# Weight products of a hybrid recurrent decoder as three fp32r products with split tiles, and heads issued in pairs

## The chip, the cores and the metric

The kernel runs on one core of a Trainium2 chip. The metric is the device time of one execution in microseconds; the median of several executions counts.

## The reference, cut to what matters

A decoder of two layers works on 288 token columns: 256 of a prompt and 32 of 8 sample sequences of 4 tokens each, which come with stored states. The model width is 1024, all in fp32. Each layer does this (cut; `prm` holds the weights):

```
u   = rmsnorm(h, norm_mix)
z   = u @ w_in                      # columns of four mixers, and of their merge gates mg
oa  = GLA(z), ob = RetNet(z), oc = gated DeltaNet(z), od = Mamba-2 SSD(z)   # chunked recurrences
proj  = einsum('blnv,nvd->blnd', stack(oa, ob, oc, od), w_branch)
gates = sigmoid(mg.reshape(B_, L, 4, D_MODEL))
h  += sum(gates * proj, axis=2) @ w_out
u   = rmsnorm(h, norm_ffn)
h  += (silu(u @ wg) * (u @ wu)) @ wd          # layer 0: one dense block of 2816
h  += top-2-of-8 experts of the same shape    # layer 1
h  += sigmoid(rmsnorm(h, norm_ple) @ ple_w_gate) * (p[i] @ ple_w_proj)   # layer-input gate
```

Besides the output, the new states of the four mixers are returned for the prompt and for every sample sequence.

## The kernel before

Activations lie transposed: 128 rows of a model block on the partitions, the 288 tokens along the free axis, `KD` = 8 such blocks. Every weight comes in tiles of 128 x 1024 fp32 (512 KB), each of which feeds eight matmuls of 128 x 128 weights by 288 columns into one PSUM bank. `TABLE` lists the tiles in the order in which they are used: for a layer 46 tiles `z` (input columns of the mixers GLA, RET, GDN and SSD: 12, 12, 12 and 10), 32 `mg` (merge gates, 8 for each mixer), 16 `br` (branch projections, 4 for each) and 8 `out`; then in layer 0 22 pairs `gate` and `up` and 22 `down`; at the end of each layer 2 `pproj` and 8 `pgate`. The 528 tiles of the experts are streamed by code of their own, which already splits each tile into a high and a low fp32r part (ACT copies it to fp32r, DVE subtracts that from the tile) and multiplies with three products (L1199 to L1201, L1221 to L1223).

Nothing is scheduled by a compiler. Each engine has its own instruction list, and semaphores tie them together. SP starts the load of tile t into slot t % `RING` of a ring of 11 slots, as soon as PE has used tile t - 11 (`tile_done`). PE does a mixer's recurrence step by step; where a step has to wait for the other engines, it fills in weight tiles. The table `SLOTS` says how many tiles stand at each of these places, and `fill(L, n, s)` issues them on PE (`stream`, matmul at L696 for z, mg, pgate and out, at L703 for br) and, at the same place of their own lists, on ACT (`take`, which copies the bank out: L1291 to L1299) and on DVE (`branch_tile`, L1598 and L1601, which multiplies br banks by their gates). So all three engines are in order, and a wait at the head of one list holds all that stands behind it. Tile t uses bank t % 2 of PSUM, so PE may start tile t when tile t - 2 is taken.

While RET's tiles run, br tiles of the mixer before (GLA) are filled in, and so on: the first places of each mixer hold the four br tiles of the last one. GDN and SSD begin with a convolution on DVE (four operations L1786 to L1792 for one block of 128 channels) and ACT (L1397, a tanh for each block), 8 blocks in GDN and 6 in SSD; the transposes on PE (L783) can only begin behind it.

For one head, `outputs(hh)` in `core` issues three matmuls of the prompt and then, for each of the 8 sample sequences, one with the head's 64-row state as weights and 4 columns (L834). GLA, RET and GDN put the even head of two in rows 0 to 63 of the array and the odd head in rows 64 to 127; SSD's two heads of a pair share the rows and write other output columns. `states(L, n)` does, head by head, two prompt matmuls (L881, L882) and eight of 32 x 64 by 128 (L889) with masks that POOL has written (L2252), or in SSD one of 512 columns (L886). GDN's `ks` products (L1020) have 4 columns too.

## Time and profile before

| | |
|---|---|
| median of 3 runs | 2867.82 us (2862.18 to 2868.1) |
| profiled execution | 2866.38 us |
| its span | 2864.4 us |
| mean granted TensorE clock | 0.922 of 2.4 GHz |
| busy: PE, DVE, ACT, POOL | 2684.9, 1309.7, 826.8, 169.4 us |
| matmul records | 12532 |

The busy time of an engine is the union of its instructions' times. An fp32 matmul appears as two records in the trace, so a tile of eight matmuls has 16 records, while an fp32r matmul has one. The granted clock is 1 at 2.4 GHz and 0.5 at 1.2 GHz.

### The profile page before, as it was taken

To read this page: it belongs to the slowest core of one execution; us is meant where nothing else is said; L and a number is where in the kernel's file an instruction comes from. 1 tells how busy PE (TensorE), PEld (TensorE's weight loads), DVE (VectorE), ACT (ScalarE), POOL (GpSimd) and SP (SyncE) were. 2 spreads that over 40 slices of the span, in tenths; PEclk is the share of its full clock that TensorE was granted. 3 is DMA by queue.
4 is the path that set the end of the run, shared out by engine and by line. 5 is a ranking of instruction groups with operands and counts; after the bars stand their busy time and mean duration, and the time that the engine had idled before them with its cause. 6 is when DMAs were issued, how large, how long until landed. Compare 5 with 4: busy or idle time off the path is not lost.

```text
span 2864.4 us, 34373 instructions
## 1 busy us (share of the span) xinstructions
PE 2684.9 (94%) x12532; PEld 2133.0 (74%) x12532; DVE 1309.7 (46%) x1790; ACT 826.8 (29%) x1171; POOL 169.4 (6%) x245
## 2 busy tenths in 40 slices
PE   8999979899999999999979899989999999999997
PEld 6777757777677776777757777668788788787785
DVE  1231252153311022132253243348879778888883
ACT  1110111012000001110111011026667666666661
POOL 0200101011100000110001010100000000000000
PEclk8989989788999998998889878879999999999999
DMA  5213321021334342323231121139889888898872
GB/s 218 96 67 119 113 73 59 30 93 48 112 125 138 134 138 82 110 74 105 81 112 59 37 71 52 51 144 335 300 309 322 305 329 300 309 341 290 306 284 85
DMA packets 122256, 455.29 MB, mean 159 GB/s; under 512 B 14024, under 2 KB 14442, under 8 KB 119730
## 3 DMA queue, kind: packets, MB, share of 16 engines
q1 hardware_dynamic: 118818, 433.51, 42.7%
q0 software_dynamic: 3344, 20.41, 1.9%
q8 instruction: 72, 1.18, 0.2%
q14 instruction: 22, 0.18, 0.0%
HBM read 442.87 MB, written 11.00 MB: 158 GB/s over the span
## 4 chain that ended last, share of the span: by engine, by line
PE 82%; DVE 10%; issue 5%; ACT 2%; DVEq 0%; DMA 0%; ACTq 0%; POOL 0%; POOLq 0%
PE ps L696 27%; PE ps L1098 6%; DVE weights_low L2093 4%; PE ps L1199 4%; PE ps L703 3%; PE ps L1201 3%; PE ps L1200 3%; PE ps L1105 3%; PE ps L834 3%; PE ps L1221 3%; PE ps L1222 3%; PE ps L1223 3%; PE ps L1172 3%; PE ps L889 2%; PE ps L726 1%
## 5 line engine op out<-in xcount | busy, mean ns | idle before, releaser
L696 PE MATMUL ps<-u,ring 128*128 128x288 f32 x2752 | 756.6, 437 | 10.8 <-DVE u L1612 7.9
L696 PEld LDWEIGHTS ps<-u,ring 128*128 128x128 f32 x2752 | 558.7, 206 | 179.9 <-issue 17.9
L2093 DVE TENSOR_TENSOR weights_low<-ring,weights_high 128x1024 fp32r<-128x1024 f32 x528 | 609.9, 1217 | 44.7 <-ACT weights_high L1507 40.6
L1507 ACT ACTIVATE weights_high<-ring 128x1024 fp32r<-128x1024 f32 x528 | 514.0, 1052 | 98.4 <-PE ps L1201 49.4
L1199 PE MATMUL ps<-weights_high,rows_high 128*128 128x512 f32 (+1 forms) x768 | 294.5, 383 | 28.0 <-DVE weights_low L2093 27.6
L1201 PE MATMUL ps<-weights_high,rows_low 128*128 128x512 f32 (+1 forms) x768 | 285.6, 372 | 0.0
L1200 PE MATMUL ps<-weights_low,rows_high 128*128 128x512 f32 (+1 forms) x768 | 285.1, 371 | 0.0
L1199 PEld LDWEIGHTS ps<-weights_high,rows_high 128*128 128x128 f32 x768 | 144.1, 188 | 62.6 <-DVE weights_low L2093 44.0
L1098 PE MATMUL ps<-u,ring 128*128 128x288 f32 x704 | 172.6, 409 | 3.2 <-DVE u L1612 3.2
L1098 PEld LDWEIGHTS ps<-u,ring 128*128 128x128 f32 x704 | 134.7, 191 | 41.1 <-issue 3.6
L1201 PEld LDWEIGHTS ps<-weights_high,rows_low 128*128 128x128 f32 x768 | 144.1, 188 | 20.9
L1200 PEld LDWEIGHTS ps<-weights_low,rows_high 128*128 128x128 f32 x768 | 144.4, 188 | 18.8
L703 PE MATMUL ps<-arena,ring 128*128 128x288 f32 x512 | 138.5, 431 | 9.3 <-DVE arena L1598 9.3
L1221 PE MATMUL ps<-weights_high,hidden_high 128*128 128x512 f32 x352 | 138.5, 394 | 0.0
L1222 PE MATMUL ps<-weights_low,hidden_high 128*128 128x512 f32 x352 | 137.0, 389 | 0.0
L1223 PE MATMUL ps<-weights_high,hidden_low 128*128 128x512 f32 x352 | 137.0, 389 | 0.0
L703 PEld LDWEIGHTS ps<-arena,ring 128*128 128x128 f32 x512 | 103.0, 203 | 45.2 <-issue 15.9
L1291 ACT ACTIVATE arena<-ps 128x288 f32<-128x288 f32 x64 | 26.3, 411 | 377.8 <-PE ps L696 377.7
L1299 ACT ACTIVATE arena<-ps 128x288 f32<-128x288 f32 x64 | 26.3, 410 | 281.5 <-PE ps L696 281.5
L1105 PE MATMUL ps<-arena,ring 128*128 128x288 f32 x352 | 85.6, 406 | 0.6 <-DVE arena L1992 0.6
L834 PE MATMUL ps<-arena 64*128 64x4 f32 (+1 forms) x640 | 84.5, 261 | 0.0
L834 PEld LDWEIGHTS ps<-arena 64*128 64x128 f32 (+1 forms) x640 | 81.0, 214 | 2.0
(363 smaller groups left out, 2887.3 us busy)
## 6 DMA issues: line engine op xcount, KB each, us to landing
ring<-in_stream SPq DMA_DIRECT2D x818, 512.0 KB, 4.9
arena<-in_state POOLq DMA_DIRECT2D x8, 1024.0 KB, 7.3
state_s<-arena POOLq DMA_DIRECT2D x8, 1024.0 KB, 4.3
const<-in_const SPq DMA_DIRECT2D x1, 2884.5 KB, 14.3
h<-in_x SPq DMA_DIRECT2D x1, 1152.0 KB, 5.2
y<-u POOLq DMA_DIRECT2D x1, 1152.0 KB, 4.4
state_p<-arena POOLq DMA_DIRECT2D x8, 128.0 KB, 4.1
expert_memory<-in_ple POOLq DMA_DIRECT2D x2, 288.0 KB, 3.0
```

What stands on the lines that cost most here:

```text
L696: last = mm(bank(t % 2)[:, 0:TOK], w[k], (acc if kind == "out" else u)[:, k, :], start=k == 0, stop=k == KD - 1)
L703: last = mm(bank(o)[:, 0:TOK], w[4 * o + k], src, start=k == 0, stop=k == 3)
L834: last = mm(o[:, 256 + 4 * b:260 + 4 * b], st_of(n)[kr, pair, b, :], qg[kr, pair, 4 * b:4 * b + 4], start=False, stop=True, skip_group_che ...
L1098: last = mm(bank(M + 2 * (f % 2) + (kind == "up"))[:, 0:TOK], w[k], u[:, k, :], start=k == 0, stop=k == KD - 1)
L1199: mm(out, xg_high[:, k, :], hi, start=k == 0, stop=False)
L1200: mm(out, xg_high[:, k, :], lo, start=False, stop=False)
L1201: last = mm(out, xg_low[:, k, :], hi, start=False, stop=k == KD - 1)
L1221: mm(out, e_high[:, f, :], hi, start=f == 0, stop=False)
L1222: mm(out, e_high[:, f, :], lo, start=False, stop=False)
L1223: last = mm(out, e_low[:, f, :], hi, start=False, stop=f == NF - 1)
L1507: A(w_high[:, o // 4, o % 4].rearrange("p k c -> p (k c)"), w, ACT.Copy).then_inc(w_high_ready, 1)
L2093: tt(lo, w, hi.bitcast(F32), ALU.subtract).then_inc(w_low_ready, 1)
```

## The change

Four things change.

1. z, mg, gate, up, down and pgate tiles (238 of the 290) are multiplied as three fp32r products, high by high, high by low and low by high, in `product`. ACT copies each such tile into one of `HELD` = 3 buffers `tiles_high` (`high(q)`) and DVE writes the rest to `tiles_low` (`low(q)`); PE waits for `tile_low`. The input u is split the same way behind five of the norms, and so is the hidden block of the dense stage. The br, out and pproj tiles stay fp32.
2. The plain stream's ring has 5 slots in place of 11. The slot of a split tile is free once `low` has read it, that of a br, out or pproj tile once PE has used it. `split_after` writes `high(q)` into ACT's list behind tile max(that of split tile q - 3, t - 5), and `low(q)` into DVE's list at the next tile. The experts keep 11 slots.
3. Heads are issued in pairs: `outputs` and `states` do two heads, with the sample matmuls alternating between them, and `ks` goes over sequences first and heads second.
4. Memory is laid out anew: `u` shares `acc`, the decay table of RET is loaded by POOL in each layer, expert buffers reuse those of the split, layer 1's p block is loaded later.

The diff, cut to its core:

```diff
-REGION = 28464
+RING, ERING, HELD, TILE = 5, 11, 3, 1024
...
+SPLIT = [t for t, x in enumerate(PLAIN) if x[0] in ("z", "mg", "gate", "up", "down", "pgate")]
+Q_OF = {t: q for q, t in enumerate(SPLIT)}
+NORM_AT = {0: 0, 1: 1, 2: 2, 3: 3, 5: 4}
+def split_after():
+    out = {}
+    for q, t in enumerate(SPLIT):
+        key = max(SPLIT[q - HELD] if q >= HELD else -1, t - RING, -1)
+        if t >= EXPERT_AT and key < EXPERT_AT:
+            key = "tail"
+        out.setdefault(key, []).append(q)
+    return out
+DUE = split_after()
...
+                    if t - RING in Q_OF:
+                        sp.wait_ge(tile_low, Q_OF[t - RING] + 1)
+                    elif t >= RING:
                         sp.wait_ge(tile_done, t - RING + 1)
...
+            def product(out, x, uh, ul, norm_k=None):
+                t = T_OF[x]
+                q = Q_OF[t]
+                pe.wait_ge(tile_low, q + 1)
+                hi, lo = [[y[:, q % HELD, P * i:P * i + P] for i in range(KD)] for y in (t_high, t_low)]
+                if norm_k is None:
+                    for k in range(KD):
+                        mm(out, hi[k], uh[:, k, :], start=k == 0, stop=False)
+                        mm(out, hi[k], ul[:, k, :], start=False, stop=False)
+                        last = mm(out, lo[k], uh[:, k, :], start=False, stop=k == KD - 1)
+                    return last
+                for k in range(KD):
+                    pe.wait_ge(u_high_ready, KD * NORM_AT[norm_k] + k + 1)
+                    mm(out, hi[k], uh[:, k, :], start=k == 0, stop=False)
+                    mm(out, lo[k], uh[:, k, :], start=False, stop=False)
+                for k in range(KD):
+                    pe.wait_ge(u_low_ready, KD * NORM_AT[norm_k] + k + 1)
+                    last = mm(out, hi[k], ul[:, k, :], start=False, stop=k == KD - 1)
+                return last
...
+                if kind in ("z", "mg", "pgate"):
+                    bank_is_free(t, t % 2)
+                    first = {("z", 0, 0): 3 * L, ("pgate", 0, 0): 3 * L + 2}.get((kind, n, b))
+                    last = product(bank(t % 2)[:, 0:TOK], x, u_high, u_low, first)
+                    last.then_inc(tile_done, 1)
+                    return
...
+                def outputs(h0):
+                    gh = L * NHEAD + HBASE[n] + h0
+                    pe.wait_ge(pt_ready, gh + 2)
+                    taken = gh - 2 if n == SSD and h0 >= 4 else (gh if n != SSD else gh - h0)
+                    if taken > 0:
+                        pe.wait_ge(o_taken, taken)
+                    if h0 == 0:
                         pe.wait_ge(qg_ready, m + 1)
                         pe.wait_ge(state_in, 16 * (m + 1))
+                    two = []
+                    for hh in (h0, h0 + 1):
+                        half, pair = half_pair(n, hh)
+                        orow = slice(64 * (hh % 2), 64 * (hh % 2) + 64) if n == SSD else slice(0, P)
+                        two.append((slice(64 * half, 64 * half + 64), pair,
+                                    bank(M + 4 + ((hh // 2) if n == SSD else hh) % 2)[orow, :], pt[:, hh % 4, :],
+                                    [vtok[0:nt, b, dv * hh:dv * hh + dv] for b, (t0, nt) in enumerate(TB)]))
+                    for kr, pair, o, p, v in two:
+                        mm(o[:, 0:256], v[0], p[:, 0:256], start=True, stop=True)
+                        mm(o[:, 128:256], v[1], p[:, 256:384], start=False, stop=True, skip_group_check=True)
+                        mm(o[:, 256:288], v[2], p[0:32, 384:416], start=False, stop=False, skip_group_check=True)
                     for b in range(NSEQ):
+                        for i, (kr, pair, o, p, v) in enumerate(two):
+                            last = mm(o[:, 256 + 4 * b:260 + 4 * b], st_of(n)[kr, pair, b, :],
+                                      qg[kr, pair, 4 * b:4 * b + 4], start=False, stop=True, skip_group_check=True)
+                            if b == NSEQ - 1:
+                                last.then_inc(o_ps, 1)
...
+                for h0 in range(0, HEADS[n], 2):
+                    gh = L * NHEAD + HBASE[n] + h0
+                    two = []
+                    for hh in (h0, h0 + 1):
+                        half, pair = half_pair(n, hh)
+                        two.append((slice(64 * half, 64 * half + 64), pair, slice(64 * hh, 64 * hh + 64),
+                                    vtok[:, :, dv * hh:dv * hh + dv], masks[0:32, 512 * (hh % 2):512 * (hh % 2) + 512]))
+                    for r, pair, kc, v, mk in two:
+                        for b in range(2):
+                            mm(bank(M + 4)[r, dv * pair:dv * pair + dv], kdec[:, b, kc], v[:, b], start=b == 0, stop=b == 1)
+                    pe.wait_ge(masked_ready, gh + 2)
                     if n == SSD:
+                        for r, pair, kc, v, mk in two:
+                            mm(bank(M + pair)[r, :], kdec[0:32, 2, kc], mk, start=True, stop=True).then_inc(masked_used, 1)
+                        continue
+                    for b in range(NSEQ):
+                        for r, pair, kc, v, mk in two:
                             last = mm(bank(M + 2 * pair + b // 4)[r, dv * (b % 4):dv * (b % 4) + dv],
                                       mk[:, 64 * b:64 * b + 64], v[0:32, 2], start=True, stop=True)
+                            if b == NSEQ - 1:
+                                last.then_inc(masked_used, 1)
...
-                for hh in range(4):
-                    r = slice(64 * (hh % 2), 64 * (hh % 2) + 64)
-                    for b in range(NSEQ):
+                for b in range(NSEQ):
+                    for hh in range(4):
+                        r = slice(64 * (hh % 2), 64 * (hh % 2) + 64)
...
+                    q = Q_OF[T_OF[("down", L, 0, f)]]
+                    pe.wait_ge(hid_low_ready, f + 1)
+                    pe.wait_ge(tile_low, q + 1)
                     for k in range(KD):
-                        last = mm(bank(k)[:, 0:TOK], w[k], hid[:, f, :], start=f == 0, stop=f == NF - 1)
+                        out = bank(k)[:, 0:TOK]
+                        hi, lo = [y[:, q % HELD, P * k:P * k + P] for y in (t_high, t_low)]
+                        mm(out, hi, hid_high[:, f, :], start=f == 0, stop=False)
+                        mm(out, hi, hid_low[:, f, :], start=False, stop=False)
+                        last = mm(out, lo, hid_high[:, f, :], start=False, stop=f == NF - 1)
...
+            def high(q):
+                t = SPLIT[q]
+                act.wait_ge(slot_in[t % RING], 16 * (t // RING + 1))
+                if q >= HELD:
+                    act.wait_ge(tile_done, SPLIT[q - HELD] + 1)
+                A(t_high[:, q % HELD, :], ring[:, (t % RING) * TILE:(t % RING + 1) * TILE], ACT.Copy).then_inc(tile_high, 1)
+            def highs(key):
+                for q in DUE.get(key, []):
+                    high(q)
             def fill(L, n, s):
                 for x in FILL[L][n][s]:
                     take(x)
+                    highs(T_OF[x])
...
+                if k in NORM_AT:
+                    for b in range(KD):
+                        act.wait_ge(u_ready, KD * k + b + 1)
+                        A(u_high[:, b, :], u[:, b, :], ACT.Copy).then_inc(u_high_ready, 1)
...
+            def low(q):
+                t = SPLIT[q]
+                dve.wait_ge(tile_high, q + 1)
+                tt(t_low[:, q % HELD, :], ring[:, (t % RING) * TILE:(t % RING + 1) * TILE],
+                   t_high[:, q % HELD, :].bitcast(F32), ALU.subtract).then_inc(tile_low, 1)
+            def lows(key):
+                for q in DUE.get(key, []):
+                    low(q)
             def fill(L, n, s):
                 for x in FILL[L][n][s]:
+                    lows(T_OF[x] - 1)
...
+                if k in NORM_AT:
+                    for b in range(KD):
+                        dve.wait_ge(u_high_ready, KD * NORM_AT[k] + b + 1)
+                        tt(u_low[:, b, :], u[:, b, :], u_high[:, b, :].bitcast(F32), ALU.subtract).then_inc(u_low_ready, 1)
...
                         ALU.mult).then_inc(hid_ready, 1)
-                    if f - 1 > 0:
-                        dve.wait_ge(hid_ready, f - 1)
+                    dve.wait_ge(hid_ready, f + 1)
+                    cp(hid_high[:, f, :], hid[:, f % 2, :]).then_inc(dve_step, 1)
+                    dve.wait_ge(dve_step, steps.next())
+                    tt(hid_low[:, f, :], hid[:, f % 2, :], hid_high[:, f, :].bitcast(F32), ALU.subtract).then_inc(hid_low_ready, 1)
+                    lows(T_OF[("up", L, 0, f)])
```

ACT's list at the start of GDN's convolution in layer 0 (`L1291` is `take` of an mg tile, `L1397` and `L1400` the convolution's tanh). Before:

```order
L1291 ACT_TABLE_LOAD
L1291 ACTIVATE arena<-ps 128x288 x7
L1397 ACTIVATE arena<-arena 128x312 x5
L1400 ACTIVATE arena<-arena 128x1152
L1397 ACTIVATE arena<-arena 128x312 x2
```

The same place now (`L1370` is `take`, `L1346` is `high`, `L1484` and `L1487` the tanh):

```order
L1346 ACTIVATE tiles_high<-ring 128x1024
L1370 ACTIVATE arena<-ps 128x288 x3
L1346 ACTIVATE tiles_high<-ring 128x1024 x2
L1484 ACTIVATE arena<-arena 128x312 x2
L1346 ACTIVATE tiles_high<-ring 128x1024
L1484 ACTIVATE arena<-arena 128x312 x3
```

Two of the copies of tiles now stand ahead of tanh operations; they are those of z tiles 1 and 2 of SSD, whose slots are those of the first two br tiles of RET.

DVE's list there, before (`L1714` and `L1715` take RET's states, `L1786` to `L1792` are the convolution of a block, `L1774` and `L1776` its end):

```order
L1714 COPY arena<-ps 128x256
L1715 TENSOR_TENSOR arena<-arena,ps 128x2048
L1786 TENSOR_SCALAR arena<-arena,pv 128x312
L1788 SCALAR_TENSOR_TENSOR arena<-arena,pv 128x312
L1790 SCALAR_TENSOR_TENSOR arena<-arena,pv 128x312
L1792 SCALAR_TENSOR_TENSOR arena<-arena,pv 128x312
```

And now (`L1688` is `low`):

```order
L1688 TENSOR_TENSOR tiles_low<-ring,tiles_high 128x1024 x2
L1836 COPY arena<-ps 128x256
L1837 TENSOR_TENSOR arena<-arena,ps 128x2048
L1688 TENSOR_TENSOR tiles_low<-ring,tiles_high 128x1024 x3
L1908 TENSOR_SCALAR arena<-arena,pv 128x312
L1910 SCALAR_TENSOR_TENSOR arena<-arena,pv 128x312
```

The subtractions stand between the mixer's own operations on DVE.

PE's list at the outputs of GDN's heads in layer 0 (`L726` scores, `L830` to `L832` prompt, `L834` sample sequences). Before, for one head:

```order
L726 MATMUL ps<-arena 32x32
L830 MATMUL ps<-arena 128x256
L831 MATMUL ps<-arena 128x128
L832 MATMUL ps<-arena 128x32
L834 MATMUL ps<-arena 128x4 x8
```

Now, for two heads (`L785` scores, `L891` to `L893` prompt, `L896` sample sequences):

```order
L785 MATMUL ps<-arena 32x32
L891 MATMUL ps<-arena 128x256
L892 MATMUL ps<-arena 128x128
L893 MATMUL ps<-arena 128x32
L891 MATMUL ps<-arena 128x256
L892 MATMUL ps<-arena 128x128
L893 MATMUL ps<-arena 128x32
L896 MATMUL ps<-arena 128x4 x16
```

The 16 sample matmuls of two heads now follow each other, one of each head in turn.

## Rows read from the trace of the kernel before

**Rows 1.** Windows by stage: us, busy (records) of PE, PEld, DVE, ACT, POOL, clock, DMA.

```profile
0.00:787.00 787.00, 723.05 (x3464) 561.26 (x3465) 246.89 (x418) 109.32 (x225) 83.18 (x121) 0.88 0.27 94
787.00:1044.00 257.00, 256.38 (x1050) 200.33 (x1051) 22.72 (x51) 10.32 (x23) 0.00 (x0) 0.99 0.39 132
1044.00:1878.00 834.00, 772.42 (x3647) 596.90 (x3645) 269.15 (x464) 115.39 (x236) 85.69 (x123) 0.88 0.23 77
...
1990.00:2812.00 822.00, 794.90 (x3759) 660.43 (x3758) 677.61 (x709) 526.01 (x607) 0.00 (x0) 1.00 0.85 308
```

**Rows 2.** Timeline of PE in GDN: start, us, engine, line, operation, tiles, records.

```profile
500.88 4.05 PE L696 MATMUL ps<-u,ring 128*128 128x288 f32 x16
504.77 1.95 PE L996 MATMUL ps<-arena 128*128 128x128 f32 x16
```

**Rows 3.** Timeline of PE in the experts: fp32r products of 384 and 512 columns.

```profile
2199.99 0.33 PE L1201 MATMUL ps<-weights_high,rows_low 128*128 128x384 f32 x1
...
2200.51 0.33 PE L1201 MATMUL ps<-weights_high,rows_low 128*128 128x384 f32 x1
...
2229.95 0.39 PE L1221 MATMUL ps<-weights_high,hidden_high 128*128 128x512 f32 x1
...
2230.63 0.39 PE L1221 MATMUL ps<-weights_high,hidden_high 128*128 128x512 f32 x1
```

**Rows 4.** Groups of PE by form: records, busy us, mean ns of one, idle before.

```profile
L696 PE MATMUL ps<-u,ring 128*128 128x288 f32 x2752 | 756.6, 437 | 10.8 <-DVE u L1612 7.9 <-DVE arena L1598 2.8
...
L889 PE MATMUL ps<-arena 32*64 32x128 f32 x384 | 63.2, 329 | 0.0
...
L834 PE MATMUL ps<-arena 64*128 64x4 f32 x384 | 60.8, 287 | 0.0
...
L834 PE MATMUL ps<-arena 64*64 64x4 f32 x256 | 23.7, 221 | 0.0
...
L1020 PE MATMUL ps<-arena 64*128 64x4 f32 x128 | 19.8, 327 | 0.0
```

**Rows 5.** Timeline of PE: one z or mg tile right behind GDN's outputs.

```profile
584.26 6.72 PE L696 MATMUL ps<-u,ring 128*128 128x288 f32 x16
```

**Rows 6.** Window of GDN's outputs, columns as in rows 1.

```profile
560.00:585.00 25.00, 25.00 (x98) 22.40 (x99) 1.29 (x4) 1.86 (x5) 0.58 (x1) 0.50 0.00 1
```

**Rows 7.** Timeline of PE in GLA: L913 alternates heads, L834 keeps to one.

```profile
128.46 1.26 PE L913 MATMUL ps<-arena 64*128 64x128 f32 x16
...
162.09 1.94 PE L834 MATMUL ps<-arena 64*128 64x4 f32 x16
```

**Rows 8.** The page: costliest groups and DMA issues, the split and the loads.

```profile
L2093 DVE TENSOR_TENSOR weights_low<-ring,weights_high 128x1024 fp32r<-128x1024 f32 x528 | 609.9, 1217 | 44.7 <-ACT weights_high L1507 40.6
L1507 ACT ACTIVATE weights_high<-ring 128x1024 fp32r<-128x1024 f32 x528 | 514.0, 1052 | 98.4 <-PE ps L1201 49.4
...
ring<-in_stream SPq DMA_DIRECT2D x818, 512.0 KB, 4.9
```

**Rows 9.** Timeline: starts of RET, GDN and SSD up to the first transposes (L783).

```profile
239.75 0.66 PE L783 MATMUL ps<-const,arena 128*128 128x128 f32 x4 [3.21 <-DVE arena L1892]
...
341.95 22.23 PE L696 MATMUL ps<-u,ring 128*128 128x288 f32 x80
...
409.42 1.11 PE L783 MATMUL ps<-const,arena 128*128 128x128 f32 x4 [11.82 <-DVE arena L1907]
...
639.02 0.66 PE L783 MATMUL ps<-const,arena 128*128 128x128 f32 x4 [1.98 <-DVE arena L1776]
```

**Rows 10.** Timeline: DVE operations of a norm, and the first gate tile.

```profile
786.22 3.52 DVE L1612 SCALAR_TENSOR_TENSOR u<-h,pv,arena 128x288 f32<-128x288 f32 x8
...
786.89 8.47 PE L1098 MATMUL ps<-u,ring 128*128 128x288 f32 x27 [3.22 <-DVE u L1612]
```

**Rows 11.** Timeline of POOL: masks for the states of GLA.

```profile
201.17 1.03 POOL L2252 TENSOR_TENSOR arena<-arena,const 32x512 f32<-32x512 f32 x1 [12.46 <-PE ps L889]
203.64 2.04 POOL L2252 TENSOR_TENSOR arena<-arena,const 32x512 f32<-32x512 f32 x1 [1.43 <-PE ps L889]
```

More of the change, by code:

```diff
@@ L293, in build @@
         slot_in = [semaphore(f"slot{j}_in") for j in range(RING)]
[L294 removed]
+        expert_slot_in = [semaphore(f"expert_slot{j}_in") for j in range(ERING)]
         const_in = semaphore("const_in")
@@ L823, in outputs @@
                         pe.wait_ge(qg_ready, m + 1)
                         pe.wait_ge(state_in, 16 * (m + 1))
-                    o = bank(M + 4 + ((hh // 2) if n == SSD else hh) % 2)[orow, :]
-                    if n == SSD and hh >= 4:
-                        pe.wait_ge(o_taken, gh - gh % 2 - 2)
-                    p = pt[:, hh % 4, :]
-                    v = [vtok[0:nt, b, dv * hh:dv * hh + dv] for b, (t0, nt) in enumerate(TB)]
-                    mm(o[:, 0:256], v[0], p[:, 0:256], start=True, stop=True)
@@ L1089, in dense @@
                 for f in range(NF):
-                    for kind in ("gate", "up"):
+                    for g, kind in enumerate(("gate", "up")):
                         if f - 1 > 0:
                             pe.wait_ge(hid_ready, f - 1)
-                        x = (kind, L, 0, f)
-                        w = weights(x)
-                        for k in range(KD):
-                            if f == 0 and kind == "gate":
-                                pe.wait_ge(u_ready, KD * (3 * L + 1) + k + 1)
-                            last = mm(bank(M + 2 * (f % 2) + (kind == "up"))[:, 0:TOK], w[k], u[:, k, :],
-                                      start=k == 0, stop=k == KD - 1)
-                        last.then_inc(tile_done, 1)
+                        first = 3 * L + 1 if f == 0 and g == 0 else None
+                        product(bank(M + 2 * (f % 2) + g)[:, 0:TOK], (kind, L, 0, f), u_high, u_low, first).then_inc(tile_done, 1)
                 pe.wait_ge(hid_ready, NF)
                 for f in range(NF):
-                    w = weights(("down", L, 0, f))
+                    q = Q_OF[T_OF[("down", L, 0, f)]]
+                    pe.wait_ge(hid_low_ready, f + 1)
+                    pe.wait_ge(tile_low, q + 1)
                     for k in range(KD):
-                        last = mm(bank(k)[:, 0:TOK], w[k], hid[:, f, :], start=f == 0, stop=f == NF - 1)
+                        out = bank(k)[:, 0:TOK]
[3 more added lines that the diff above has]
+                        last = mm(out, lo, hid_high[:, f, :], start=False, stop=f == NF - 1)
                     last.then_inc(tile_done, 1)
@@ L1473, in dense @@
                     A(tanh_t[:, f % 2, :], bank(M + 2 * (f % 2))[:, 0:TOK], ACT.Tanh, scale=0.5).then_inc(tanh_ready, 1)
+                    highs(T_OF[("gate", L, 0, f)])
+                    highs(T_OF[("up", L, 0, f)])
+                for f in range(NF):
+                    highs(T_OF[("down", L, 0, f)])
             def experts(L):
@@ L1561, in _ @@
                 ssd(L)
+                for b in range(4):
+                    highs(T_OF[("br", L, 3, b)])
+                for b in range(KD):
+                    highs(T_OF[("out", L, 0, b)])
                 norm(3 * L + 1)
                 dense(L) if L % 2 == 0 else experts(L)
+                if L == 1:
+                    highs("tail")
                 norm(3 * L + 2)
@@ L1655, in prep @@
                 last.then_inc(logd_ready, 1)
+                for b in range(4, ZBLOCKS[0] - 1):
+                    lows(T_OF[("z", L, 0, b)])
                 dve.wait_ge(cum_ps, L + 1)
@@ L2174, in _ @@
                     dve.wait_ge(const_in, 16)
+                for b in range(4):
+                    lows(T_OF[("z", L, 0, b)])
                 prep(L)
@@ L2189, in _ @@
                     square(3 * L + 1, b)
+                lows(T_OF[("out", L, 0, KD - 1)])
                 norm(3 * L + 1, "norm_ffn")
                 dense(L) if L % 2 == 0 else experts(L)
+                if L == 1:
+                    lows("tail")
                 norm(3 * L + 2, "norm_ple")
+                for b in range(2):
+                    lows(T_OF[("pproj", L, 0, b)])
                 for b in range(KD):
```

200 lines of the change are left out of this document (101 added, 99 removed).

## The prediction, made before the changed kernel ran

> **What bounds the kernel now.** I read first the windows by stage, then the groups of instructions on PE, then the timeline where PE stands still. In both mixer stages PE is busy 723.05 of 787 and 772.42 of 834 us, in the dense stage 256.38 of 257, in the experts 794.9 of 822 [rows 1]. DVE is busy a third of a mixer stage and ACT a seventh. So PE's own list sets the time, except at short places where PE waits for a chain on DVE and ACT. The granted clock is 0.88 in the mixer stages and 0.99 and 1.00 in the dense stage and the experts [rows 1]: part of the mixers' work runs at 1.2 GHz, for example all of 560 to 585 us, GDN's outputs, and a tile right behind them that takes 6.72 us in place of 4.05 [rows 5, 6]. The largest group is the z, mg and pgate tiles, 756.6 us [rows 4]; the dense stage's 257 us are tiles of the same shape.
>
> **The product of a tile.** At 2.4 GHz a tile starts 3.89 us ahead of what follows it (500.88 to 504.77) [rows 2]: 8 matmuls of 486 ns, two records each. The fp32r products that the changed kernel uses do not occur with 288 columns. Nearest are those of the experts: three issues of 512 columns take 0.68 us (2229.95 to 2230.63), 227 ns each, and three of 384 columns 0.52 us (2199.99 to 2200.51), 173 ns each [rows 3]. A straight line through the two gives 133 ns for 288, hence 400 ns for three products against 486 for one fp32 matmul. That saves 85 ns on each of 238 x 8 = 1904 matmuls: 1904 x 0.085 = **-162 us** (mixers 156 tiles -106, dense 66 tiles -45, pgate 16 tiles -11). A tile takes 3.2 us then. If a product cost as much at 288 columns as at 384, three would take 519 ns and the term would be +63; that end I give little, since 512 and 384 columns already differ by a quarter.
>
> Of fp32 the Trainium skill says ("FP8 and Floating Point Precision", TensorE Precision Notes) that true fp32 takes four passes through the array, high and low parts of both operands multiplied with each other. By that page three one-pass products are three quarters of 486, 364 ns, an estimate that would make this term -231 us. The rows of fp32r here stand above it, and I keep to the line through them.
>
> Records at 1.2 GHz gain more. The group has 172 tiles in 756.6 us; at 4.05 us each (with the last record's end) they would be 697, so 60 us are slow clock [rows 2, 4]. At 2.67 us lost by a tile like that of [rows 5] this is 22 tiles, 180 matmuls; the lower part of a range, 126, follows with the full doubling of 486 ns. At half clock the saving is 170 ns and not 85, and the tile is shorter by as much again: I take 126 x 0.16 = **-20**.
>
> **Pairs.** L834 on 64 rows of 128 columns is 60.8 us busy and L1020 19.8 [rows 4]. They have 4 columns and are issued every 110 ns: (1.94 - 0.29) / 15. L913, which alternates between the row halves, takes (1.26 - 0.29) / 15 = 65 ns [rows 7], where 0.29 is one record's own time [rows 4]. So pairs on opposite rows take 0.5 (two at a time) to 0.59 of the time: -33 to -40, taken **-36**. L889 (63.2) and SSD's L834 (23.7) [rows 4] pair heads that share the rows and differ in columns. No row of before shows such a pair: bounds 0 and -43; taken halfway, **-22**.
>
> **What is new on the path.** ACT's copy of a tile takes 1052 ns and DVE's subtraction 1217 ns in the experts, a load lands 4.9 us after its issue [rows 8]. Summed, 238 of each are 250 us on ACT and 290 on DVE, with room beside 2685 us of PE; what costs is only where they stand.
>
> - First tile behind a norm. PE starts on u_high, but u_low needs eight more DVE operations behind the eight of the norm (3.52 us for eight; the first gate tile starts 0.67 us after the first of them now [rows 10]). So the last u_low is there 7.0 us after the norm's first u, and the tile ends some 0.2 later; now it ends 0.67 + 3.89 = 4.6 after it. That is 2.7 us for each of the three norms that have no other tile to hide it: **+8**.
> - Slots held by br tiles. With 5 slots, tile t's load starts when tile t - 5 is done. For six tiles of each layer, the second and third z (or mg) tile behind the br tiles, t - 5 is a br tile, and such a tile is free only when PE has used it. From there: 4.9 (load) + 1.05 (copy), and 1.22 (subtraction) until PE may start; meanwhile the copy waits at the head of ACT's list with the convolution's tanh behind it, and the subtraction holds DVE's convolution. In RET the load falls beside DVE's rope chain, for which PE waits 3.21 us already [rows 9]: +4.3. In GDN, 341.95 to 409.42 [rows 9] is a DVE and ACT chain, in which PE idles 11.82 us at its end: the shorter tiles (7 x 0.68 = 4.8) bring nothing there, and two copies (5.95 each) less 3.9 of a br tile lengthen it by 8: +12.8. In SSD, where PE waits 1.98 us for the convolution before 639.02 [rows 9], it has little beside br tiles, so both delays of 7.2 are exposed: +14.4. Together 31.5 in a layer, **+63**. Bounds: 0, if the loads run ahead of the tanh chain, and 2 x 6 x 7.2 = 86.
> - Masks. `states` now waits for both masks of a pair, each 1.03 to 2.04 us on POOL [rows 11], and writes the next pair only when the last is used: about 1.6 for each of 8 mixers' states, **+13**.
> - GLA's levels and places where DVE stands in `low` while PE waits for a mixer step: two layers, four such steps of 1.2: **+10**. Places where tiles follow each other: take, copy, subtraction and waits make 0.41 + 1.05 + 1.22 = 2.7 of 3.2 us, so each small delay shows: **+10**.
> - Clock. Behind the 11.82 us wait the first four matmuls of L783 take 1.11 us against 0.66 elsewhere [rows 9]: a long wait is followed by 1.2 GHz. Twelve new waits of 4 to 8 us, of which half do that for some 5 us: **+15** (0 to 36).
>
> Dense: 6.4 us of PE for a pair of tiles, DVE 4.4, ACT 2.6 and loads 1 MB, less than half of what the experts' stage moves in that time; PE stays the bound. Experts: nothing changes.
>
> **Sum.** -162 - 20 - 36 - 22 = -240; + 8 + 63 + 13 + 10 + 10 + 15 = +119; total -121. The profiled execution has 2866.4 us and the median of the runs lies 1.4 higher. 2867.8 - 121 = **2747**.
>
> **Rivals.**
> - Splitting eats the mixers' gain. If each `low` of the 156 mixer tiles (1.22 us) stands ahead of an operation that PE waits for, that is +190 in place of the five small terms and the slots (121 less the norm's 8, so 111): -240 + 8 + 190 = -42, **2826**. For it: DVE is in order, and mixers are chains over DVE. Against: DVE is idle two thirds of that time, and the fill tiles stand where PE has steps to wait for.
> - The loads are early enough and the clock no worse: only +8 and +13 remain, -219, **2649**. For it: PE idles in three of these places now, so part of the delay is free. Against: the order of ACT's list, with the copies ahead of the tanh.
> - The column pairs bring nothing, **2769**. L889 and SSD's L834 load their weights into the same rows. The Trainium skill states ("TensorE: Matmul & The Clock Gate", Part 3, What overlaps and what doesn't) that a weight load overlaps running matmuls only when its row group differs. No row of before pairs columns, so I give this three in ten inside the forecast, whose range holds it.
> - Slower. The lookahead is gone: three buffers let a copy start only when tile q - 3 is done, and it is behind mixer operations in two lists. If copy and subtraction, 2.27 us, are exposed for all 156 tiles, that is +354: -240 + 8 + 354 = +122, **2990**. From 1.5 us a tile (232 / 156) on the change loses. For it: 2.7 of 3.2 us are full where tiles follow each other. Against: most tiles of GLA and GDN stand alone between steps of several us.
>
> **How the numbers follow.** The forecast gets 0.65, the first rival 0.16, the second 0.13, the slower one 0.06. The forecast's own range, from its terms' bounds, is 2700 to 2795. The range for 8 in 10 is 2655 to 2828: it leaves out the slower rival, half of the second, and the upper part of the first. Two measurements of this kernel can differ by 0.2% (6 us) with nothing changed; faster by more than that has 0.93, no change 0.01, slower 0.06.
>
> **What would show it.** Tiles of 24 records every 3.2 us (products every 133 ns); the dense stage down to some 212 us with PE busy throughout; GDN's outputs in half the time; waits of 4 to 7 us on PE for `tile_low`, or for the convolution, at the second and third tile behind br tiles. The prediction fails if three products take as long as the fp32 matmul, if PE's waits for `tile_low` stand at all mixer tiles and not at twelve, or if the mixers fall to 1.2 GHz more often than before.

## The result, and the profile after

The changed kernel takes 2745.98 us (median of 4 runs, 2738.75 to 2753.48) against 2865.0 of the kernel before on the same chip: a ratio of 0.9586, 95% interval 0.9552 to 0.962. The forecast was 2747. The head and the engines of the profiled execution:

```profile
span 2748.3 us, 38217 instructions
...
PE 2462.7 (90%) x14436; PEld 2124.5 (77%) x14436; DVE 1628.5 (59%) x2112; ACT 1074.4 (39%) x1450; POOL 178.8 (7%) x247
```

PE is busy 222 us less and idle 106 us more (2748.3 - 2462.7 = 285.6, before 2864.4 - 2684.9 = 179.5). These are roughly the two columns of the forecast's sum, -240 and +119; the experts, which the forecast put at 0, add 16 us to the busy time. The stages of both kernels, cut at the same places (first gate tile, end of the last down tile, end of layer 1's mixers, experts from the second to the last); columns as in [rows 1], first before, then after:

```profile
0.00:786.90 786.90, 722.95 (x3464) 561.16 (x3464) 246.79 (x418) 109.32 (x225) 83.18 (x121) 0.88 0.27 94
786.90:1046.00 259.10, 258.26 (x1056) 201.49 (x1056) 22.94 (x52) 10.32 (x23) 0.00 (x0) 0.99 0.39 132
1046.00:1872.50 826.50, 770.61 (x3639) 595.85 (x3639) 264.18 (x456) 114.89 (x235) 85.69 (x123) 0.88 0.23 77
...
2001.60:2800.90 799.30, 773.42 (x3668) 643.50 (x3666) 658.88 (x683) 516.94 (x596) 0.00 (x0) 1.00 0.85 310
```

```profile
0.00:754.50 754.50, 638.05 (x4087) 555.09 (x4088) 348.73 (x508) 189.65 (x316) 87.59 (x122) 0.85 0.28 96
754.50:969.30 214.80, 214.05 (x1584) 212.92 (x1584) 119.91 (x167) 79.82 (x96) 0.00 (x0) 0.99 0.47 155
969.30:1744.00 774.70, 664.03 (x4327) 577.36 (x4327) 372.13 (x556) 201.61 (x336) 90.13 (x123) 0.88 0.25 87
...
1874.00:2684.00 810.00, 789.36 (x3669) 645.79 (x3667) 657.88 (x681) 517.92 (x598) 0.00 (x0) 1.00 0.85 305
```

The dense stage gives 44.3 us, with PE busy for 214.05 of its 214.80, the mixer stages 32.4 and 51.8. In the mixer stages PE is busy 85 and 107 us less, but it idles 52 and 55 us more. The experts, whose products the change leaves as they were, take 10.7 us longer: PE is busy 15.9 us more and idle 5.2 less.

The products behind each other at 2.4 GHz, which answer to [rows 2, 3] (their pitch is the time from the start of one to the start of the next):

```profile
30.06 0.29 PE L717 MATMUL ps<-u_high,tiles_low 128*128 128x288 f32 x1
...
30.46 0.29 PE L717 MATMUL ps<-u_high,tiles_low 128*128 128x288 f32 x1
```

Three products take 0.40 us (30.06 to 30.46), 133 ns each, as the line through the experts' rows gave. The first tile behind the norm of the dense stage:

```profile
754.52 0.37 PE L721 MATMUL ps<-u_high,tiles_high 128*128 128x288 f32 x1 [3.70 <-ACT u_high L1386]
...
758.33 1.98 PE L725 MATMUL ps<-u_low,tiles_high 128*128 128x288 f32 x8
```

It runs from 754.52 to 760.14, where the next tile starts: 5.6 us where a later tile takes 3.2.

The groups of the paired heads, which answer to [rows 4], and two of them in the timeline, which answer to [rows 7]; 32 records stand now where 16 stood:

```profile
L954 PE MATMUL ps<-arena 32*64 32x128 f32 x384 | 32.1, 333 | 11.7 <-POOL arena L2390 11.7
...
L896 PE MATMUL ps<-arena 64*128 64x4 f32 x384 | 31.1, 290 | 0.0
...
L896 PE MATMUL ps<-arena 64*64 64x4 f32 x256 | 11.9, 221 | 0.0
L1086 PE MATMUL ps<-arena 64*128 64x4 f32 x128 | 11.6, 314 | 0.0
```

```profile
163.29 2.34 PE L896 MATMUL ps<-arena 64*128 64x4 f32 x32
...
194.81 1.96 PE L954 MATMUL ps<-arena 32*64 32x128 f32 x32
```

In the kernel before, one head's states:

```profile
597.32 1.96 PE L889 MATMUL ps<-arena 32*64 32x128 f32 x16
```

Row pairs (L896 on 128 columns, L1086) are 42.7 us busy and were 80.6. Column pairs (L954, L896 on 64 columns) are 44.0 and were 86.9. Both kinds run two at a time.

The br tiles' group in the kernel before (records, busy us, mean ns, idle before):

```profile
L703 PE MATMUL ps<-arena,ring 128*128 128x288 f32 x512 | 138.5, 431 | 9.3 <-DVE arena L1598 9.3
```

And what PE waited for in the changed kernel (line, releaser: us in total, times, longest):

```profile
PE ps L762 <- DVE arena L1712: 59.6, 8, 9.3
PE ps L842 <- DVE arena L2029: 27.8, 2, 13.9
...
PE ps L721 <- ACT u_high L1386: 13.2, 3, 5.7
PE ps L954 <- POOL arena L2390: 11.7, 6, 2.7
...
PE ps L974 <- DVE ps L1926: 8.0, 2, 4.0
...
PE ps L950 <- POOL arena L2390: 3.5, 4, 1.0
PE ps L979 <- DVE arena L1962: 3.4, 2, 1.7
```

L762 is the br tile. Its wait for DVE's `branch_tile` was 9.3 us in all, and is 59.6 with 4.6 more in another row. L954 and L950 wait 15.2 us for POOL's masks, before nothing. L721 are the first tiles behind norms, which waited 11.1 us before. L974 and L979 are GLA's levels, which waited for nothing before.

SSD's start in layer 0 shows what the 59.6 us are: first ACT, then PE (records of the z and mg tiles left out):

```profile
570.64 0.45 ACT L1484 ACTIVATE arena<-arena 128x312 f32<-128x312 f32 x1
578.80 1.06 ACT L1346 ACTIVATE tiles_high<-ring 128x1024 fp32r<-128x1024 f32 x1 [7.71 <-DMA ring<-in_stream]
579.76 0.45 ACT L1484 ACTIVATE arena<-arena 128x312 f32<-128x312 f32 x1
592.61 1.06 ACT L1346 ACTIVATE tiles_high<-ring 128x1024 fp32r<-128x1024 f32 x1 [12.40 <-DMA ring<-in_stream]
```

```profile
569.19 4.04 PE L762 MATMUL ps<-arena,ring 128*128 128x288 f32 x16
582.54 6.79 PE L762 MATMUL ps<-arena,ring 128*128 128x288 f32 x16 [9.31 <-DVE arena L1712]
596.35 10.59 PE L762 MATMUL ps<-arena,ring 128*128 128x288 f32 x32 [7.03 <-DVE arena L1712]
613.04 0.66 PE L842 MATMUL ps<-const,arena 128*128 128x128 f32 x4 [2.92 <-DVE arena L1898]
```

The first br tile ends at 573.2. Only then is the slot of mg tile 1 free; its load lands at 578.8. ACT's copy (L1346) waits 7.71 us for it, with the tanh (L1484) behind it, DVE's convolution waits for the tanh, `branch_tile` stands behind that, and PE waits 9.31 us for the bank. Then the same once more: 7.03 us. From the end of GDN's states to L842 it is 48.3 us in layer 0 and 48.1 in layer 1 (29.3 both before); in GDN's start 77.9 and 75.9 (67.4 and 67.3), in RET's 28.9 and 29.2 (27.2 and 27.0). The six starts together take 308 us and took 247.

### The profile page after: what moved, and what is told of

It is laid out like the page before. It is cut to its first block, busy times and chain, and to the rows that moved or that the text cites. A ratio compares the mean times of both kernels' runs of the same rounds, so it can differ in the third digit from the quotient of the medians.

```text
span 2748.3 us, 38217 instructions
## 1 busy us (share of the span) xinstructions
PE 2462.7 (90%) x14436; PEld 2124.5 (77%) x14436; DVE 1628.5 (59%) x2112; ACT 1074.4 (39%) x1450; POOL 178.8 (7%) x247
## 4 chain that ended last, share of the span: by engine, by line
PE 77%; DVE 11%; issue 5%; ACT 4%; DMA 1%; POOL 1%; DVEq 0%; SPq 0%; ACTq 0%; POOLq 0%
PE ps L715 9%; PE ps L717 8%; PE ps L716 8%; PE ps L762 5%; DVE weights_low L2220 4%; PE ps L1265 4%; PE ps L1267 3%; PE ps L1266 3%; PE ps L1287 3%; PE ps L1288 3%; PE ps L1289 3%; PE ps L1238 3%; PE ps L756 2%; PE ps L896 2%; DMA ring<-in_stream 1%
## 5 line engine op out<-in xcount | busy, mean ns | idle before, releaser
L715 PE MATMUL ps<-u_high,tiles_high 128*128 128x288 f32 x1688 | 535.1, 317 | 2.6 <-DVE arena L1712 2.6
L716 PE MATMUL ps<-u_low,tiles_high 128*128 128x288 f32 x1688 | 521.3, 309 | 0.0
L717 PE MATMUL ps<-u_high,tiles_low 128*128 128x288 f32 x1688 | 519.1, 307 | 0.0
L1688 DVE TENSOR_TENSOR tiles_low<-ring,tiles_high 128x1024 fp32r<-128x1024 f32 x238 | 291.7, 1229 | 268.7 <-ACT tiles_high L1346 267.6
L715 PEld LDWEIGHTS ps<-u_high,tiles_high 128*128 128x128 f32 x1688 | 340.8, 202 | 12.7 <-issue 6.7
L1346 ACT ACTIVATE tiles_high<-ring 128x1024 fp32r<-128x1024 f32 x238 | 250.7, 1054 | 245.9 <-DMA ring<-in_stream 155.9
L716 PEld LDWEIGHTS ps<-u_low,tiles_high 128*128 128x128 f32 x1688 | 341.0, 202 | 0.6
L717 PEld LDWEIGHTS ps<-u_high,tiles_low 128*128 128x128 f32 x1688 | 340.3, 202 | 0.0
L2220 DVE TENSOR_TENSOR weights_low<-expert_ring,weights_high 128x1024 fp32r<-128x1024 f32 x288 | 334.3, 1217 | 4.9 <-ACT weights_high L1597 2.2
L1265 PE MATMUL ps<-weights_high,u_high 128*128 128x512 f32 (+1 forms) x768 | 297.6, 388 | 23.2 <-DVE weights_low L2220 22.6
L2220 DVE TENSOR_TENSOR weights_low<-ring,weights_high 128x1024 fp32r<-128x1024 f32 x240 | 280.1, 1217 | 42.9 <-ACT weights_high L1597 41.8
L762 PE MATMUL ps<-arena,ring 128*128 128x288 f32 x512 | 155.9, 470 | 64.2 <-DVE arena L1712 59.6
L762 PEld LDWEIGHTS ps<-arena,ring 128*128 128x128 f32 x512 | 113.2, 224 | 106.7 <-issue 71.7
```

Of the source, the lines that this page charges most:

```text
L715: mm(out, hi[k], uh[:, k, :], start=k == 0, stop=False)
L716: mm(out, hi[k], ul[:, k, :], start=False, stop=False)
L717: last = mm(out, lo[k], uh[:, k, :], start=False, stop=k == KD - 1)
L762: last = mm(bank(o)[:, 0:TOK], w[4 * o + k], src, start=k == 0, stop=k == 3)
L1265: mm(out, xg_high[:, k, :], hi, start=k == 0, stop=False)
L1346: A(t_high[:, q % HELD, :], ring[:, (t % RING) * TILE:(t % RING + 1) * TILE], ACT.Copy).then_inc(tile_high, 1)
```

## The experiments

Theory (slots): the products give what their pitch says, the pairs what their busy times say, and what the mixers lose they lose at the six tiles of a layer whose slot a br tile holds, by the place of the copy in ACT's list. Rival (DVE's list): the subtractions lie on the path wherever they stand. A second rival: column pairs bring nothing.

**The copies two tiles later.** The load has two br tiles of time before ACT comes to the copy. The edit moves 27 copies: of the twelve tiles, of the six tiles ahead of them in the starts, and of the first dense and layer-input gate tiles.

```diff
-        key = max(SPLIT[q - HELD] if q >= HELD else -1, t - RING, -1)
+        key = max(SPLIT[q - HELD] if q >= HELD else -1, t - 3, -1)
```

> Only the place of `high` and `low` in ACT's and DVE's lists changes: two tiles later for the tiles whose slot a br tile holds (and for the first gates), so that the load has two branch tiles of time and the convolution's tanh stands ahead of the copy. Theory (slots): the loss in the mixers sits at these six tiles of a layer, in the starts of GDN (77.9 and 76.0 us up to the first transposes, 67.4 before) and SSD (48.3 and 48.1, 29.3 before); then these go back to some 65 and 32 us, PE's wait at the br tiles falls from 64 to under 20 us, and the time by 45 to 60, to some 2690. Rival (DVE's list): the subtractions themselves hold the chain, wherever they stand; then the time falls by no more than 15.

2694.45 us, ratio 0.9424 (0.939 to 0.9457): 51 us faster than the changed kernel by the medians, 46 by the two ratios. SSD's start in layer 0, ACT and PE:

```profile
546.15 0.46 ACT L1484 ACTIVATE arena<-arena 128x312 f32<-128x312 f32 x1 [1.25 <-DVE arena L1914]
550.52 1.06 ACT L1346 ACTIVATE tiles_high<-ring 128x1024 fp32r<-128x1024 f32 x1 [3.91 <-DMA ring<-in_stream]
554.58 1.06 ACT L1346 ACTIVATE tiles_high<-ring 128x1024 fp32r<-128x1024 f32 x1 [3.00 <-DMA ring<-in_stream]
```

```profile
541.07 4.04 PE L762 MATMUL ps<-arena,ring 128*128 128x288 f32 x16
547.20 4.12 PE L762 MATMUL ps<-arena,ring 128*128 128x288 f32 x16 [2.09 <-DVE arena L1712]
551.51 4.12 PE L762 MATMUL ps<-arena,ring 128*128 128x288 f32 x16 [0.18 <-DVE arena L1712]
558.33 4.12 PE L762 MATMUL ps<-arena,ring 128*128 128x288 f32 x16 [2.70 <-DVE arena L1712]
569.69 0.73 PE L842 MATMUL ps<-const,arena 128*128 128x128 f32 x4 [4.06 <-DVE arena L1898]
```

The copies wait 3.9 and 3.0 us in place of 7.7 and 12.4, PE 2.1, 0.2 and 2.7 us at the br tiles in place of 9.3 and 7.0. The start of SSD is 33.2 us now in layer 0 and 34.9 in layer 1, still 4 and 6 more than before the change; that of GDN is 63.6 and 67.8, about what it was (67.4 and 67.3). The six starts together go from 308 back to 250 us: 58 of the 60 us between the two profiled spans (2748.3 and 2688.5) lie there. PE's waits:

```profile
PE ps L842 <- DVE arena L2029: 30.1, 2, 15.0
...
PE ps L762 <- DVE arena L1712: 16.7, 8, 3.3
```

The br tiles' wait falls from 59.6 to 16.7. The theory holds, the rival does not. What is left in GDN's start is the wait for the chain that stood there before ([rows 9]), 15 us in each layer where it was 11.8. This kernel is faster than both.

**Each mixer subtraction twice.** 156 x 1.23 = 192 us more on DVE.

```diff
                 dve.wait_ge(tile_high, q + 1)
+                if PLAIN[t][0] in ("z", "mg"):
+                    tt(t_low[:, q % HELD, :], ring[:, (t % RING) * TILE:(t % RING + 1) * TILE],
+                       t_high[:, q % HELD, :].bitcast(F32), ALU.subtract).then_inc(dve_step, 1)
+                    dve.wait_ge(dve_step, steps.next())
```

> DVE does the subtraction of each of the 156 z and mg tiles twice, 1.23 us more each. Theory (slots): a subtraction lies on the path only at the twelve tiles held back by br tiles and at a few steps of the chains, so +20 to +50 us. Rival (the first of the prediction): each subtraction stands ahead of something that PE waits for, +190 us.

2794.32 us, ratio 0.9761 (0.9745 to 0.9777): +48, a quarter of the 192. The wait at br tiles grows from 64.2 us (59.6 and 4.6) to 80.4 (7.1 of it in another row):

```profile
PE ps L762 <- DVE arena L1716: 73.3, 10, 11.0
```

It is as if one subtraction in four lay on the path. The first rival of the prediction, all of them, is out.

**Heads apart.** The alternation is undone in the outputs, the states and ks, for example:

```diff
-                    for b in range(NSEQ):
-                        for i, (kr, pair, o, p, v) in enumerate(two):
+                    for kr, pair, o, p, v in two:
+                        for b in range(NSEQ):
...
-                    pe.wait_ge(masked_ready, gh + 2)
...
+                    for i, (r, pair, kc, v, mk) in enumerate(two):
+                        pe.wait_ge(masked_ready, gh + 1 + i)
+                        for b in range(NSEQ):
```

> The matmuls of two heads no longer alternate: within a pair the eight sample matmuls of the first head come before those of the second, states waits for each mask by itself, and ks goes head by head. The forecast's prices give +58, of which 22 for the heads that differ in columns only. The busy times of the changed kernel (L954 32.1 against 63.2, L896 31.1 and 11.9 against 60.8 and 23.7, L1086 11.6 against 19.8) give +81 less some 8 for the masks. The rival that column pairs bring nothing gives +36 and no difference in the busy time of L954.

2808.65 us, ratio 0.9816 (0.9796 to 0.9835): +63, between the +58 of the forecast's prices and the +73 of the busy times.

**Only the columns apart.** The same edit in the states, and in the outputs of SSD alone.

> The changed kernel, with the alternation undone only where the two heads share the rows and write other columns: the sample matmuls of the states (L954, L950) and of SSD's outputs; GLA, RET and GDN keep theirs in the outputs and ks. By the busy times of the changed kernel (L954 32.1 against 63.2 before, SSD's L896 11.9 against 23.7) +43 less 15 for the waits for masks: +28 us. By the forecast's half price +22 - 13 = +9. If column pairs bring nothing, -13 (the masks' waits alone come back).

2771.31 us, ratio 0.9681 (0.9657 to 0.9704): +25.

```profile
L955 PE MATMUL ps<-arena 32*64 32x128 f32 x384 | 58.7, 349 | 0.0
...
L896 PE MATMUL ps<-arena 64*128 64x4 f32 x384 | 29.9, 285 | 0.0
...
L896 PE MATMUL ps<-arena 64*64 64x4 f32 x256 | 20.0, 221 | 0.0
```

The column pairs' groups go up to 58.7 and 20.0 us and the row pairs stay at 29.9. Column pairs bring 25 us net of the masks' waits, the row pairs the remaining 38. The rival that column pairs bring nothing is out.

**The third product left out.** The kernel leaves out low weights by high input for all tiles, so its output lacks that part.

```diff
-                        mm(out, hi[k], ul[:, k, :], start=False, stop=False)
-                        last = mm(out, lo[k], uh[:, k, :], start=False, stop=k == KD - 1)
+                        last = mm(out, hi[k], ul[:, k, :], start=False, stop=k == KD - 1)
```

> Leaves out the third product (low weights by high input) of all split tiles but the first behind the second part of a norm; copies and subtractions stay. If PE is still the bound everywhere, 1904 x 133 ns = -253 us. If the mixers are bound by the chains on ACT and DVE, only the dense stage and the layer-input gate gain: -60 to -80, with DVE as the next bound in the dense stage. The theory (slots) lies between: in the starts of RET, GDN and SSD nothing is gained (9 tiles of a layer), elsewhere all: about -200.

2529.87 us, ratio 0.8841 (0.8824 to 0.8857): -216 of 253. From SSD's last state in layer 0 to the last down tile (272.9 and 204.6 us) it gives 68 of 70, in the mixers of both layers with layer 0's layer-input gate tiles (pgate) 144 of 175. PE's own work is the bound in most places, and the br tiles' wait, which has nothing to do with the products, stays:

```profile
PE ps L760 <- DVE arena L1709: 56.5, 8, 7.3
```

**The small ring alone, in the kernel before.** The plain stream uses 5 of the 11 slots; SP's loop over its loads is written out for that.

```diff
-                    if t >= RING:
-                        sp.wait_ge(tile_done, t - RING + 1)
+                    if t >= PRING:
+                        sp.wait_ge(tile_done, t - PRING + 1)
```

> The kernel before with one part of the change alone: the plain stream uses 5 slots in place of 11 (the experts keep theirs), fp32 products, heads apart. Theory (slots): the small ring costs only together with the copies, because then a load is on the path of ACT's and DVE's lists; here a tile has four tiles of 3.9 us between its load and its use, against 4.9 us of load, so 0 to +6 us. Rival: the ring itself is too small, loads are late at the br tiles whatever reads them: +20 us or more. The experts' products of 512 columns should stay at 227 ns, since their code and memory are those of before; if they go to 234, the pitch hangs on something ahead of them.

2859.27 us, ratio 0.9994 (0.9981 to 1.0008): nothing. The br tiles (L694 here) wait as before:

```profile
PE ps L694 <- DVE arena L1589: 9.3, 8, 3.3
```

So five slots alone cost nothing while PE reads the tiles itself. In the changed kernel the wait comes with the copies behind the loads.

**The experts' 11 us.** The products of 512 columns in the changed kernel:

```profile
2201.72 0.40 PE L1287 MATMUL ps<-weights_high,tiles_high 128*128 128x512 f32 x1
...
2202.42 0.39 PE L1287 MATMUL ps<-weights_high,tiles_high 128*128 128x512 f32 x1
```

Three issues take 0.70 us, 234 ns each, where the kernel before has 227 [rows 3]; those of 384 columns stay at 173. The 2592 products of 512 columns, in gate and up as in down, make that some 18 us; PE's shorter waits for `weights_low` (22.6 us against 27.6) give 5 of it back. In the kernel with the later copies the steps settle into a series of seven, 231, 234, 235, 233, 232, 238 and 237 ns, and their mean is the same whether DVE and ACT are busy or not. Five kernels with the later copies and one of before look for the reason. First the experts' weights 512 bytes further on:

```diff
+        slotrow = sb("slot_rows", PLACES)[:, :]
         w_high = sb("weights_high", SPLITS * TILE, F32R)[:, :].rearrange("p (m i k c) -> p m i k c", m=2, i=4, k=KD)
```

> As the run with the later copies, and the experts' buffers weights_high and weights_low lie 512 bytes further on in each partition (a small tensor is allocated ahead of them). The experts' products of 512 columns follow each other every 227 ns before the change and every 234 in all runs since; nothing in their instructions was changed but addresses. Theory (address of the moving weights): the pitch changes with this shift, and goes back to 227 if it is their place modulo 1 KB: -11 us. Rivals: the address of the stationary rows (then no change here), or the loads' target (no change here).

Then 1536 bytes further on, in the same way with a tensor of 384 columns:

> As the run with the later copies, with weights_high and weights_low 1536 bytes further on, so that their place modulo 4 KB is that of the kernel before. If the experts' products of 512 columns hang on the place of the moving weights modulo 2 or 4 KB, they go back from 234 to 227 ns and the time falls by 11 us, to some 2683. If not, nothing changes, and the place of the weights is ruled out at four positions.

Then the stationary rows of the down stage moved by 20 KB:

```diff
-        ring = sb("ring", RING * TILE)
         th_t, tl_t = sb("tiles_high", HELD * TILE, F32R), sb("tiles_low", HELD * TILE, F32R)
...
+        ring = sb("ring", RING * TILE)
```

> As the run with the later copies, with tiles_high and tiles_low, whose memory the experts use for their hidden rows, allocated ahead of the ring: they move by 20 KB, weights_high and weights_low stay. Theory (address of the moving weights): no change, 234 ns everywhere. Rival (address of the stationary rows): the products of the down stage (L1287 to L1289) change, those of gate and up (stationary u_high) do not.

Then the experts' slots of the ring ahead of the weights:

```diff
+        more_ring = sb("expert_ring", (ERING - RING) * TILE)
         w_high = sb("weights_high", SPLITS * TILE, F32R)[:, :].rearrange("p (m i k c) -> p m i k c", m=2, i=4, k=KD)
```

> As the run with the later copies, with the six expert slots of the ring allocated ahead of weights_high and weights_low: these move by 24 KB, their place modulo 1 KB stays. Theory (address of the moving weights modulo 1 KB): 234 ns stay. Rival (which region the loads write beside the weights): the pitch changes, for some slots at least.

Then the loop elsewhere in PE's program:

```diff
+                for _ in range(5):
+                    pe.wait_ge(pos_ready, 1)
                 pe.wait_ge(zeroed, 1)
```

> As the run with the later copies, with five waits on PE (on a semaphore that has long been reached) ahead of the experts' loop, so that the loop's instructions lie elsewhere in PE's program. If the pitch of 512 columns hangs on where the loop's code lies, it changes from 234 ns; if not, it stays.

And the kernel before again:

> The kernel before once more, for one profile on another day of the chip: if the 227 ns of the experts' products belong to the kernel, they are seen again; if the chip or its state of that day made them, they read 234 here and the 11 us that the changed kernel lost in the experts are none of the change.

The first four take 2699.04, 2696.35, 2696.35 and 2699.0 us (ratios 0.9421, 0.9432, 0.9427 and 0.9441, none clear of 0.9424), the fifth 2704.52 in one run: 234 ns in all five. The kernel before (2866.62 in one run) and its version with the small ring keep 227. Busy time and mean of one group of the down stage in the ring version of before, and in the version shifted by 1536 bytes:

```profile
L1213 PE MATMUL ps<-weights_low,hidden_high 128*128 128x512 f32 x352 | 137.0, 389 | 0.0
```

```profile
L1288 PE MATMUL ps<-weights_high,tiles_high 128*128 128x512 f32 x352 | 141.1, 401 | 0.0
```

So it belongs to the changed kernel and not to a chip, and it is neither the place of the moving weights (four places), nor that of the down stage's stationary rows, nor where the loop lies in the program. No run moved the stationary rows of gate and up (`u_high`, `u_low`), whose products have the 234 too. What it is stays open.

## Why the prediction held, point by point

The total is right to 1 us. The mechanism of each large term was seen, but that the sum is so close is luck: the column pairs gave some 20 us more than forecast, while the records at 1.2 GHz gave some 14 less and the experts took 11. Two sums of the prediction are off. The terms that the first rival replaces are 119 - 8 = 111, not 121 - 8. And of the 160 ns behind the -20 only 85 follow from its rows (170 less the 85 that -162 holds already), which would be -11 and a total of 2756.

- **Products, -162.** Held: 133 ns; the dense stage gave 44.3 (forecast 45 less 2.7 for its first tile). By the rule of four passes for fp32 in the Trainium skill ("FP8 and Floating Point Precision", TensorE Precision Notes) the estimate was 364 ns for three products; the trace shows 400 against 486, so the line through the rows was the better guide. Not all of it reached the time: the last stage, with the eight pgate tiles of layer 1, takes 64.3 us and took 63.5, since PE waits 4.8 us for ACT at its second pproj tile where it waited 1.2.
- **Records at 1.2 GHz, -20.** Mis-sized. In the group of z, mg and pgate tiles some 250 records follow each other every 479 ns in place of 243, 58 us lost; in the changed kernel some 500 products every 239 ns in place of 133, 53 us lost. A matmul there gains 156 ns more than the 86 of full speed, about the 160 that was taken, but more of them run at 1.2 GHz, and some 6 us are left.
- **Row pairs, -36.** 80.6 to 42.7 us busy: -38.
- **Column pairs, -22.** Mis-sized: 86.9 to 44.0 us, -43, the far end of the bounds. I halved it for want of a row. The rule in the Trainium skill ("TensorE: Matmul & The Clock Gate", Part 3, What overlaps and what doesn't) that weight loads overlap running matmuls only for differing row groups is not borne out here: 32 records of L954 on the same 32 rows, each with a weight load of its own, take the 1.96 us that 16 took in the kernel before (at 597.32 us of its trace).
- **First tiles, +8.** About right: in the dense stage the tile ends 6.8 us behind the norm's first u (753.4), where 7.2 was forecast and 4.6 held before.
- **Slots held by br tiles, +63.** The mechanism is shown by the run with the later copies (-51), and the ring alone costs nothing. The wait shows at another place than the prediction named: not at the split tiles (PE waits 2.6 us in all at L715), but already at the br tiles, whose banks `branch_tile` frees late. The size by place: GDN's start was forecast 8 us longer and is 10.5 and 8.6; SSD's was forecast 14.4 less two shorter tiles and is 19.0 and 18.8. There the load took 5.5 us and not 4.9, and the br tile behind the first wait took 6.79 us in place of 4.04, in part at 1.2 GHz. RET's start was forecast 4.3 and is 1.7 and 2.2 longer. In all that is 61 us, 17 of them by the clock (below); the forecast has 51 here and 15 for the clock.
- **Masks, +13.** 15.2 us of waits.
- **GLA and tight places, +20.** GLA's levels wait 11.4 us (L974, L979) that they did not wait before, where +10 was forecast. No run isolates the tight places. Doubling every mixer subtraction cost 48 us, so one subtraction in all places together costs of that order, the twelve slot tiles included.
- **Clock, +15.** The granted clock fell from 0.922 to 0.914. That is 473 us at 1.2 GHz (twice 0.086 of 2748.3) against 447. The run with the later copies shows the term: in the six starts the time at 1.2 GHz is 56 us before, 125 in the changed kernel and 58 with the later copies, and the br tiles there lose 7, 24 and 5 us to it: +17. The prediction named more 1.2 GHz in the mixers as a sign that it fails. That sign came in layer 0 (granted clock 0.85 against 0.88, some 225 us at 1.2 GHz against 191) and not in layer 1 (191 against 201); the total held all the same, since the term had allowed for it.
- **Experts, 0.** Wrong: +10.7, by the pitch of 512 columns; why the pitch changed is open.

Of the rivals, the first (each subtraction on the path) fell with the doubled subtractions, the second (loads early enough) with the waits of 7.7 and 12.4 us, and the slower one with both. Moving the copies comes near to the second: it gave 2649, and the kernel with the later copies has 2694. Of the difference 11 us are the experts', and 16.7 us of waits are still left at the br tiles (9.3 before the change); the rest was not taken apart.

## What to carry to other kernels

Where every engine works through its own list in order, an operation that needs a transfer should not stand right behind the event that starts the transfer: with the copies two tiles later the kernel took 51 us less, with the same buffers. The cost of a split product is read from the pitch of the same kind of product at other sizes, on a line (133 ns, as measured) and not in proportion (288/512 of 227 would be 128). Small matmuls on part of the array are worth alternating between opposite halves, rows (80.6 to 42.7 us) or columns (86.9 to 44.0).

## What the runs showed of the hardware

Column pairs on the same rows run two at a time (44.0 against 86.9 us). Products of 512 columns have two steady pitches, 227 ns in the kernel before and 234 in all kernels with the change, at a granted clock of 1.00 in both; those of 384 columns have one, 173. The time of one and the same kernel goes with the granted clock of the run: the runs of the kernel with the later copies have 2688.48, 2690.24, 2698.65 and 2707.78 us at 0.925, 0.923, 0.919 and 0.914, so a difference of 0.7% between single runs of this kernel can be the clock's.
